# DMA transposes for q, k and the retention output, and four gate groups held back, in a hybrid decoder layer on eight cores

## The chip, the cores and the metric

The kernel runs on all eight cores of one Trainium2 chip. Each core has its own TensorE (PE, matrix multiply into PSUM), VectorE (DVE), ScalarE (ACT), GpSimd (POOL), SyncE (SP) and 16 DMA engines. The metric is the device time in microseconds of the slowest core. The cores do not talk to each other: each computes its own tokens from its own copy of the weights.

## The reference, cut to what matters

```python
h = x @ w_in
a_u, a_v, a_z, r_q, r_k, r_v, r_z, g_a, g_b = split(h)
ya = (spatial_gating(gelu(a_u), gelu(a_v), ...) * silu(a_z)) @ w_oa
q = rotary(r_q); k = rotary(r_k)                  # 8 heads, 128 wide
ret = retention(q, k, r_v)                        # chunks of 128 tokens, v 256 wide
yb = (ret * silu(r_z)) @ w_ob
out = (sigmoid(g_a + b) * ya + sigmoid(g_b + b) * yb) @ w_out
x = layer_norm(2**0.25 * x + out)

# retention, for one head, chunk i, state R
scores = (q k^T) * decay                          # 128 x 128
out_i  = standardize(scores @ v + (q @ R) * cross_decay)
R      = R * chunk_decay + (k * w)^T v
```

x is 4 x 4096 x 2048, so four sequences; each is shared by two cores.

## The kernel before

An even core takes 17 chunks of 128 tokens of a sequence, in tiles of 9 and 8 chunks; an odd core takes the other 15 (tiles of 8 and 7) and first computes the retention state that the even core's chunks leave behind (`prefix`). For each tile the program runs six stages, all of them big matrix products with K = 2048 (16 matmuls of 128 rows into one PSUM bank, called a group): `v_stage`, `uz_stage`, `oa_stage`, `ret_stage`, `obg_stage`, `out_stage`. Weights come by POOL's queue, 512 KB a unit, into a ring of 16 slots (`w_issue`, `w_take`, `w_free`); all other transfers go by SP's queue. Instructions are issued to each engine in the order in which the Python code records them, and `Sched` adds the semaphore waits; a PSUM bank is guarded as a whole between engines.

`ret_stage` is the one that changes. Its main loop has one iteration i for each head h and chunk c, N = 8 x (9 or 8) of them, software-pipelined. In iteration i:

- `p_mm(i)`: the group that makes q, k and v of chunk c, with 512 columns, into a PSUM bank.
- `p_post(i)`: ACT copies q and k (scaled) to `q32` and v to `v`.
- `small_pe(i)`: small matmuls of earlier iterations. For i-2 the two TensorE transposes of q and k (`qkt`, from rotary) into bank 3; for i-4 k^T v (into bank 4); for i-3 the scores (from `qkT`, the transposed q and k); for i-4 the output (from `ST`, `v`, `qkT`, `Rg`) into bank 5 or 6; for i-7 the two TensorE transposes of the normed output `ybp` into bank 7.
- `small_post(i)`: ACT and DVE work behind them: the state `U`, the masked scores `ST`, the norm's statistics `mv`, its factor `rs` (ACT's square root), the normed output `ybp` for i-5, and the ACT copies of the transposes out of PSUM, into `qkT` for i-2 and into `aT` for i-7.
- `rotary(i)`: four DVE operations that write `qkt`, last of DVE's work in the iteration.

The same ring takes in four weight units at each end of a head (`w_free` behind `c == n - 1`).

Behind the loop the gate stage begins: for each of 16 column blocks `ct` a group of r_z, then tanh on ACT and two DVE operations that multiply `aT` by the gate. In its first seven groups the pipeline of the retention runs dry (the drain): each of these has `small_pe` and `small_post` of the iterations N to N+6 between the group and its gate. On ACT a square root and a tanh need different tables, so they cost table loads where they alternate.

```
b = step % 3 if step < 7 + 3 else self.next_bank()
...
if drain:
    small_pe(i)
    small_post(i)
```

Of the kernel before, what the change touches and what calls it, by code (L numbers as in the profile page):

```python
# [9 lines left out]
BF16 = mybir.dt.bfloat16  # L10
AF = mybir.ActivationFunctionType
ALU = mybir.AluOpType
# [3 lines left out]
KT = 16  # L16
NH = 8
CH = 128
# [182 lines left out]
class Prog:  # L201
# [89 lines left out]
    def load(self, key, out, in_, eng="sp", reads=(), after=()):  # L291
        self.S.op(eng, lambda e: e.dma_start(out=out, in_=in_), list(reads), [out], key=key, after=after)  # L292

    def store(self, key, out, in_, eng="sp", writes=()):
        self.S.op(eng, lambda e: e.dma_start(out=out, in_=in_), [in_], list(writes), key=key)

# [248 lines left out]
    def ret_stage(self):  # L545
        m, n = self.m, self.n
# [3 lines left out]
        N = NH * n  # L550
# [8 lines left out]
        def p_mm(i):  # L559
            h, c = divmod(i, n)  # L560
            if c == 0:
                slot[h] = self.w_take(4)
                if init:
                    if h == 0:
                        yh_load(0)
                    if h + 1 < NH:
                        yh_load(h + 1)
            b = i % 3
            s = slot[h]
            self.group(self.bank(b), [(self.xT[:, kt, c * 128:(c + 1) * 128], m.ring[:, s:s + 4, kt, :]) for kt in range(KT)])  # L570
            if c == n - 1:
                self.w_free()

        def p_post(i):
            h, c = divmod(i, n)
            b = i % 3
            q32 = m.q32[i % 3]
            self.act(q32[:, 0, :], self.bank(b)[:, 0:128], AF.Copy, scale=m.dec[:, h:h + 1])
            self.act(q32[:, 1, :], self.bank(b)[:, 128:256], AF.Copy, scale=m.dec[:, 8 + h:9 + h])
            self.act(m.v[i % 6][:], self.bank(b)[:, 256:512], AF.Copy)  # L580

        def rotary(i):
            h, c = divmod(i, n)
            q32, ta, tb = m.q32[i % 3], m.ta[i % 2], m.tb[i % 2]
            x = q32[:].rearrange("p j (e f) -> p (j e) f", e=2)
            cb = m.cs[:, c, 0:64].unsqueeze(1).to_broadcast([128, 4, 64])
            sb_ = m.cs[:, c, 64:128].unsqueeze(1).to_broadcast([128, 4, 64])
            self.tt(ta[:].rearrange("p j e f -> p (j e) f"), x, cb, ALU.mult)
            self.tt(tb[:].rearrange("p j e f -> p (j e) f"), x, sb_, ALU.mult)
            o = m.qkt[i % 6]  # L590
            self.tt(o[:, :, 0:64], ta[:, :, 0, :], tb[:, :, 1, :], ALU.subtract)
            self.tt(o[:, :, 64:128], ta[:, :, 1, :], tb[:, :, 0, :], ALU.add)

        def rg_set(i):
            h, c = divmod(i, n)
# [2 lines left out]
        def state_init(h, b):  # L598
            s = slot[h]
            ps = self.bank(b)[:, 0:256]  # L600
            self.group(ps, [(m.yh[h % 2][:, kt, :], m.ring[:, s + 2:s + 4, kt, :]) for kt in range(KT)])
            self.ts(m.U[:, h, :], ps, float(1.0 / self.gC1[h]), None, ALU.mult)

        def small_pe(i):
            a, b_, c_, y = i - 2, i - 3, i - 4, i - 7
            if 0 <= a < N:
                for j in range(2):
                    self.tr(self.bank16(3)[:, j * 128:(j + 1) * 128], m.qkt[a % 6][:, j, :])
            if 0 <= c_ < N:
                h, c = divmod(c_, n)  # L610
                if not (last and c == n - 1):
                    self.mm(self.bank(4)[:, 128:384], m.qkt[c_ % 6][:, 1, :], m.v[c_ % 6][:], True, True)
            if 0 <= b_ < N:
                self.mm(self.bank(4)[:, 0:128], m.qkT[b_ % 4][:, 1, :], m.qkT[b_ % 4][:, 0, :], True, True)
            if 0 <= c_ < N:
                ob = self.bank(5 + c_ % 2)[:, 0:256]
                self.mm(ob, m.ST[c_ % 3][:], m.v[c_ % 6][:], True, False)
                self.mm(ob, m.qkT[c_ % 4][:, 0, :], m.Rg[c_ % 3][:], False, True)
            if 0 <= y < N:
                for j in range(2):  # L620
                    self.tr(self.bank16(7)[:, j * 128:(j + 1) * 128], m.ybp[y % 4][:, j * 128:(j + 1) * 128])

        def small_post(i):
            a, b_, c_, y = i - 2, i - 3, i - 4, i - 7
            z = i - 5
            if 0 <= z < N:
                k = z % 4
                mv, r = m.mv[k], m.rs[k]
                self.rstd(r[:, 0:1], mv[:, 1:2], m.eps1)
                self.stt(r[:, 1:2], mv[:, 0:1], -1.0, r[:, 0:1], ALU.mult, ALU.mult)  # L630
            if 0 <= a < N:
                self.act(m.qkT[a % 4][:].rearrange("p j t -> p (j t)"), self.bank16(3)[:, 0:256], AF.Copy)
            if 0 <= c_ < N:
                h, c = divmod(c_, n)
                if not (last and c == n - 1):
                    self.stt(m.U[:, h, :], m.U[:, h, :], float(self.gC[h]), self.bank(4)[:, 128:384], ALU.mult, ALU.add)
            if 0 <= b_ < N:
                self.tt(m.ST[b_ % 3][:], self.bank(4)[:, 0:128], m.maskT[:], ALU.mult)
            if 0 <= c_ < N and c_ + 1 < N:
                rg_set(c_ + 1)  # L640
            if 0 <= c_ < N:
                ob = self.bank(5 + c_ % 2)[:, 0:256]
                k = c_ % 4
                self.bn(m.st6[k][:], ob)
                self.aggr(m.mv[k][:, 0:2], m.st6[k][:])
            if 0 <= z < N:
                self.act(m.ybp[z % 4][:], self.bank(5 + z % 2)[:, 0:256], AF.Identity, scale=r[:, 0:1], bias=r[:, 1:2])
            if 0 <= y < N:
                h, c = divmod(y, n)
                self.act(self.aT[:, 2 * h:2 * h + 2, c * 128:(c + 1) * 128],  # L650
                         self.bank16(7)[:, 0:256].rearrange("p (j t) -> p j t", j=2), AF.Copy)

        for i in range(N):
            h, c = divmod(i, n)
            p_mm(i)
            p_post(i)
            small_pe(i)
            if c == 1 and init:
                state_init(h, (i - 1) % 3)
            if i == 3:  # L660
                rg_set(0)
            small_post(i)
            rotary(i)


        i = N
        step = 0
        for ct in range(16):
            s = self.w_take(1)
            for (c0, k) in self.sp:  # L670
                tk = slice(c0 * CH, (c0 + k) * CH)
                drain = i < N + 7
                b = step % 3 if step < 7 + 3 else self.next_bank()
                step += 1
                ps = self.bank(b)[:, 0:k * CH]
                self.group(ps, [(m.ring[:, s, kt, :], self.xT[:, kt, tk]) for kt in range(KT)])
                if drain:
                    small_pe(i)
                    small_post(i)
                    i += 1  # L680
                th = m.zth[self.rot("zt", 4)][:, 0:k * CH]
                self.act(th, ps, AF.Tanh, scale=0.5)
                self.stt(th, th, 1.0, ps, ALU.add, ALU.mult)
                a = self.aT[:, ct, tk]
                self.stt(a, a, 0.5, th, ALU.mult, ALU.mult)
            self.w_free()

    def obg_stage(self):
# [91 lines left out]
def plan_memory(nc, es):  # L780
    m = Mem()
    top = [(nc.sbuf_base + 63) // 64 * 64]
# [30 lines left out]
    m.rs = [new("rs%d" % i, [128, 2], F32) for i in range(4)]  # L813
    m.st6 = [new("st6_%d" % i, [128, 6], F32) for i in range(4)]
    s0 = top[0]
    top[0] += 32768
    assert top[0] <= nc.sbuf_usable_end, (top[0], nc.sbuf_usable_end)
    m.left = nc.sbuf_usable_end - top[0]

# [1 line left out]
    def area(start):  # L821
        pos = [s0 + start]

        def sub(name, shape, dt):
            size = int(np.prod(shape[1:])) * ESIZE[dt]
            off = pos[0]
            pos[0] += (size + 31) // 32 * 32
            assert pos[0] <= s0 + 32768
            return at(name, shape, dt, off)
        sub.pos = pos  # L830
        return sub

    a = area(0)
# [4 lines left out]
    a = area(8192)  # L838
# [5 lines left out]
    a = area(0)  # L844
# [3 lines left out]
    a = area(0)  # L848
# [2 lines left out]
    m.tb = [a("tb%d" % i, [128, 2, 2, 64], F32) for i in range(2)]  # L851
    m.qkt = [a("qkt%d" % i, [128, 2, 128], BF16) for i in range(6)]
    m.v = [a("v%d" % i, [128, 256], BF16) for i in range(6)]
    m.qkT = [a("qkT%d" % i, [128, 2, 128], BF16) for i in range(4)]
    m.ST = [a("ST%d" % i, [128, 128], BF16) for i in range(3)]
    m.ybp = [a("ybp%d" % i, [128, 256], BF16) for i in range(4)]
    m.Rg = [a("Rg%d" % i, [128, 256], BF16) for i in range(3)]
    m.cs = a("cs", [128, NMAX, 128], F32)
    assert a.pos[0] <= s0 + 24576
    a = area(24576)  # L860
    m.zth = [a("zth%d" % i, [128, 512], F32) for i in range(4)]
    a = area(24576)
    m.yh = [a("yh%d" % i, [128, KT, 128], BF16) for i in range(2)]
    a = area(16384)
    m.oga = [a("oga%d" % i, [128, 512], F32) for i in range(2)]
    m.ogb = [a("ogb%d" % i, [128, 512], F32) for i in range(2)]
    a = area(8192)
# [197 lines left out]
```

How the kernel before makes its waits and increments, by code:

```python
    def run(self, name, e):  # L172
        waited = {}
        for o in self.streams[name]:
            need = {}
            for d in o.deps:
                p = self.ops[d]
                sid = id(p.sem)
                if waited.get(sid, 0) < p.count and (sid not in need or need[sid][1] < p.count):
                    need[sid] = (p.sem, p.count)
            for sid, (sem, c) in need.items():
                e.wait_ge(sem, c)
                waited[sid] = c
            if o.fn is None:
                continue
            ins = o.fn(e)
            if o.signal:
                ins.then_inc(o.sem, 16 if o.key is not None else 1)
```

## Time and profile before

| | |
|---|---|
| time, median of 3 runs | 2763.53 us (2761.27 to 2765.18) |
| profiled execution, its time and span | 2764.21 us and 2762.7 us |
| spans of the even cores 0, 2, 4, 6 | 2762.7, 2760.7, 2762.2, 2759.8 us |
| spans of the odd cores 1, 3, 5, 7 | 2689.6, 2691.3, 2691.9, 2699.7 us |
| busy on core 0: PE, DVE, ACT | 97%, 40%, 23% |
| mean granted TensorE clock, core 0 | 0.992 |

The profile is that of core 0, an even core; odd cores are some 70 us shorter, so the even cores set the time. The busy shares are means over all stages. In the retention loop they are another mix than in the rest, and the rows below are taken from it.

### The profile page before, as it was taken

Reading aid. Unit: us, or ns where it says so; the run is one execution under the profiler, and the core shown is the slowest. Engines: PE = TensorE matmul, PEld = TensorE weight load, DVE = VectorE, ACT = ScalarE, POOL = GpSimd, SP = SyncE. Lnnn points to the kernel's source line nnn. Section 1 sums busy time; section 2 is a strip of 40 time slices with the busy share of each in tenths; the row PEclk is TensorE's granted clock in tenths of the full one; section 3 lists DMA queues with packets and bytes.
Section 4 is the critical chain, followed back from the end, with each engine's and each line's share of the span. In section 5 each row is a group of like instructions: output and inputs, shape, how many; then the busy total and the mean of one; then the engine's idle time right before and its main releaser. Section 6 shows DMA issues by size and latency. Waiting matters only on the chain.

```text
span 2762.7 us, 41067 instructions; the slowest of 8 cores (2689.6 to 2762.7 us)
## 1 busy us (share of the span) xinstructions
PE 2691.9 (97%) x14589; PEld 1394.7 (50%) x14666; DVE 1108.6 (40%) x2685; ACT 638.1 (23%) x1516; POOL 197.3 (7%) x373
## 2 busy tenths in 40 slices
PE   5899999999999999999999999999999999999998
PEld 2356666655555666666544444444555544444443
DVE  1344442156665422222375343321566642221257
ACT  0131111045555111111101221110455621111100
POOL 2000000000000000000001000000000000000000
PEclk9999999999999999999999999999999999999999
DMA  9744434423334443333558554444243454444443
GB/s 151 147 78 76 62 62 85 66 42 62 62 62 92 70 84 68 64 71 63 117 185 202 103 92 76 71 83 77 54 78 62 83 94 84 84 69 79 82 124 130
DMA packets 65919, 241.47 MB, mean 87 GB/s; under 512 B 7472, under 2 KB 11696, under 8 KB 62128
## 3 DMA queue, kind: packets, MB, share of 16 engines
q0 software_dynamic: 56064, 193.49, 41.2%
q1 hardware_dynamic: 9648, 45.27, 4.5%
q8 instruction: 125, 2.05, 0.3%
q14 instruction: 82, 0.67, 0.1%
HBM read 413.31 MB, written 18.87 MB: 156 GB/s over the span
## 4 chain that ended last, share of the span: by engine, by line
PE 94%; DMA 3%; ACT 1%; issue 1%; DVE 1%; POOL 0%; SPq 0%; DVEq 0%; ACTq 0%; POOLq 0%
PE ps_all L236 93%; DMA xT<-xT 1%; PE ps_all L245 1%; DMA ring<-w 1%; DMA bgate<-bgate 1%; ACT L257 0%; POOL ring L292 0%; DVE xy_85 L264 0%; ACT aT L257 0%; POOL xT L292 0%; SPq L292 0%; ACT zth_122 L257 0%; DVEq L931 0%; DVE zth_123 L264 0%; DVE wsT L260 0%
## 5 line engine op out<-in xcount | busy, mean ns | idle before, releaser
L236 PE MATMUL ps_all<-xT,ring 128*128 128x384 bf16 (+1 forms) x6343 | 1202.6, 348 | 5.5 <-DVE zth_122 L264 1.8
L236 PEld LDWEIGHTS ps_all<-xT,ring 128*128 128x128 bf16 x6400 | 621.9, 98 | 538.8 <-issue 4.7
L236 PE MATMUL ps_all<-ring,xT 128*128 128x512 bf16 x3264 | 734.7, 382 | 24.1 <-DMA xT<-xT 22.5
L236 PEld LDWEIGHTS ps_all<-ring,xT 128*128 128x128 bf16 x3264 | 314.8, 98 | 386.2 <-issue 37.9
L236 PE MATMUL ps_all<-aT,ring 128*128 128x384 bf16 (+1 forms) x2541 | 482.9, 347 | 1.0
L236 PEld LDWEIGHTS ps_all<-aT,ring 128*128 128x128 bf16 x2560 | 250.1, 98 | 220.0
L292 POOL DMA_DIRECT2D ring<-w x348 | 184.4, 533 | 2434.9 <-PE ps_all L236 1926.9
L236 PE MATMUL ps_all<-ring,yT 128*128 128x512 bf16 x1088 | 235.3, 380 | 0.3 <-DMA ring<-w 0.3
L236 PEld LDWEIGHTS ps_all<-ring,yT 128*128 128x128 bf16 x1088 | 106.3, 98 | 128.9 <-issue 0.8
L275 DVE CAST yT<-ps_all 128x384 bf16<-128x384 f32 (+1 forms) x40 | 24.5, 611 | 205.7 <-PE ps_all L236 205.7
L264 DVE SCALAR_TENSOR_TENSOR ogb_130<-ogb_130,ps_all 128x384 f32<-128x384 f32 (+1 forms) x40 | 24.3, 607 | 183.4 <-PE ps_all L236 183.4
L264 DVE SCALAR_TENSOR_TENSOR ogb_129<-ogb_129,ps_all 128x384 f32<-128x384 f32 (+1 forms) x40 | 24.3, 608 | 183.2 <-PE ps_all L236 183.2
L264 DVE SCALAR_TENSOR_TENSOR uth_77<-uth_77,ps_all 128x384 f32<-128x384 f32 (+1 forms) x40 | 24.3, 608 | 137.1 <-ACT uth_77 L257 113.8
L264 DVE SCALAR_TENSOR_TENSOR uth_76<-uth_76,ps_all 128x384 f32<-128x384 f32 (+1 forms) x40 | 24.3, 608 | 131.8 <-ACT uth_76 L257 82.7
L257 ACT ACTIVATE oga_128<-ps_all,bgate 128x384 f32<-128x384 f32 (+1 forms) x40 | 24.9, 623 | 211.3 <-PE ps_all L236 211.3
L257 ACT ACTIVATE oga_127<-ps_all,bgate 128x384 f32<-128x384 f32 (+1 forms) x40 | 24.9, 623 | 204.7 <-PE ps_all L236 204.7
L257 ACT ACTIVATE yT<-ps_all 128x384 bf16<-128x384 f32 (+1 forms) x40 | 21.3, 533 | 208.3 <-PE ps_all L236 208.3
L257 ACT ACT_TABLE_LOAD x34 | 43.6, 1283 | 98.5 <-PE ps_all L236 54.3
L264 DVE SCALAR_TENSOR_TENSOR oga_128<-oga_128,yT 128x384 f32<-128x384 f32 (+1 forms) x40 | 24.4, 611 | 92.4 <-ACT oga_128 L257 92.4
L264 DVE SCALAR_TENSOR_TENSOR oga_127<-oga_127,yT 128x384 f32<-128x384 f32 (+1 forms) x40 | 24.4, 611 | 90.9 <-ACT oga_127 L257 90.9
L264 DVE SCALAR_TENSOR_TENSOR U<-U,ps_all 128x256 f32<-128x256 f32 x128 | 53.9, 421 | 4.4 <-PE ps_all L236 4.1
L257 ACT ACTIVATE aT<-ps_all 128x256 bf16<-128x256 bf16 x136 | 50.8, 373 | 4.0 <-PE ps_all L245 4.0
(227 smaller groups left out, 1884.5 us busy)
## 6 DMA issues: line engine op xcount, KB each, us to landing
ring<-w POOLq DMA_DIRECT2D x348, 512.0 KB, 6.3
xy_86<-x SPq DMA_DIRECT2D x9, 1024.0 KB, 6.7
out<-xy_86 SPq DMA_DIRECT2D x18, 512.0 KB, 3.8
xy_85<-x SPq DMA_DIRECT2D x8, 1024.0 KB, 4.9
out<-xy_85 SPq DMA_DIRECT2D x16, 512.0 KB, 2.7
xT<-xT POOLq DMA_DIRECT2D x8, 576.0 KB, 22.6
xT<-xT POOLq DMA_DIRECT2D x4, 1024.0 KB, 21.8
ring<-wv POOLq DMA_DIRECT2D x8, 256.0 KB, 19.3
```

Source lines behind the costliest of these rows:

```text
L236: return self.S.op("pe", lambda e: e.matmul(out, lhsT=l, rhs=r, start=start, stop=stop), [l, r], [out])
L245: self.S.op("pe", lambda e: e.transpose(out=out, in_=in_, identity=idt), [in_, idt], [out])
L257: self.S.op("act", lambda e: e.activation(out=out, in_=in_, func=func, **kw), rd, [out])
L264: self.S.op("dve", lambda e: e.scalar_tensor_tensor(out=out, in0=a, scalar=s, in1=b, op0=op0, op1=op1), rd, [out])
L275: self.S.op("dve", lambda e: e.tensor_copy(out=out, in_=in_), [in_], [out])
L292: self.S.op(eng, lambda e: e.dma_start(out=out, in_=in_), list(reads), [out], key=key, after=after)
```

## The change

Three things change, all in `ret_stage`.

First, the four TensorE transposes of an iteration are gone, and the two ACT copies with them. In their place SP's queue gets four DMA transposes of 128 x 128 bf16, SBUF to SBUF: two behind `rotary(i)`, from `qkt` into `qkT`, and two behind the normed output of iteration i-5, from `ybp` straight into `aT`. `qkT` has six buffers where it had four. The readers of `qkT` stay where they were, the scores at i+3 and the output at i+4.

Second, the PSUM banks are dealt anew: `p_mm` rotates over banks 0 to 3 where it had 0 to 2, and k^T v goes into bank 7 where it shared bank 4 with the scores.

Third, the drain: it has four groups where it had seven. These are computed into banks 0 to 3 and held there; `small_pe` and `small_post` of N to N+3 follow each, then `small_post(N+4)`, and only then the gates (tanh and two DVE operations) of the four held groups.

```diff
+    def dma_tr(self, key, out, in_):
+        self.S.op("sp", lambda e: e.dma_start_transpose(out=out, in_=in_), [in_], [out], key=key)
...
-            b = i % 3
+            b = i % 4
...
             self.tt(o[:, :, 64:128], ta[:, :, 1, :], tb[:, :, 0, :], ALU.add)
+            for j in range(2):
+                self.dma_tr("tq%d%d" % (j, i % 6), m.qkT[i % 6][:, j, :], o[:, j, :])
...
         def small_pe(i):
-            a, b_, c_, y = i - 2, i - 3, i - 4, i - 7
-            if 0 <= a < N:
-                for j in range(2):
-                    self.tr(self.bank16(3)[:, j * 128:(j + 1) * 128], m.qkt[a % 6][:, j, :])
...
-            if 0 <= y < N:
-                for j in range(2):
-                    self.tr(self.bank16(7)[:, j * 128:(j + 1) * 128], m.ybp[y % 4][:, j * 128:(j + 1) * 128])
...
-            if 0 <= a < N:
-                self.act(m.qkT[a % 4][:].rearrange("p j t -> p (j t)"), self.bank16(3)[:, 0:256], AF.Copy)
...
-            if 0 <= y < N:
-                h, c = divmod(y, n)
-                self.act(self.aT[:, 2 * h:2 * h + 2, c * 128:(c + 1) * 128],
-                         self.bank16(7)[:, 0:256].rearrange("p (j t) -> p j t", j=2), AF.Copy)
+                for j in range(2):
+                    self.dma_tr("ty%d%d" % (j, z % 4), self.aT[:, 2 * h + j, c * 128:(c + 1) * 128], m.ybp[z % 4][:, j * 128:(j + 1) * 128])
...
-                drain = i < N + 7
-                b = step % 3 if step < 7 + 3 else self.next_bank()
+                b = i - N if i < N + 4 else self.next_bank()
...
+                if i < N + 4:
+                    held.append((ct, c0, k, b))
                     small_pe(i)
                     small_post(i)
                     i += 1
+                    if i == N + 4:
+                        small_post(i)
+                        for g in held:
+                            gate(*g)
+                else:
+                    gate(ct, c0, k, b)
```

On PE one iteration in the middle of the loop read like this before: the group, the q and k transposes (`ident,qkt`), the four small matmuls, the output's transposes (`ident,ybp`).

```order
L236 MATMUL ps_all<-ring,xT 128x512 x16
L245 MATMUL ps_all<-ident,qkt_94 128x128 x2
L236 MATMUL ps_all<-v_104,qkt_98 128x256
L236 MATMUL ps_all<-qkT_107 128x128
L236 MATMUL ps_all<-v_104,ST_111 128x256
L236 MATMUL ps_all<-Rg_118,qkT_106 128x256
L245 MATMUL ps_all<-ident,ybp_114 128x128 x2
```

The same iteration of the changed kernel, with the group of the next behind it:

```order
L236 MATMUL ps_all<-ring,xT 128x512 x16
L236 MATMUL ps_all<-v_104,qkt_98 128x256
L236 MATMUL ps_all<-qkT_111 128x128
L236 MATMUL ps_all<-v_104,ST_113 128x256
L236 MATMUL ps_all<-Rg_120,qkT_110 128x256
L236 MATMUL ps_all<-ring,xT 128x512 x16
```

Four instructions of 128 columns are gone from each iteration; the rest stands in the same order.

On SP nothing stood in the loop before. Now the queue alternates there between the q and k transposes of iteration i and the output's transposes of iteration i-4 (`aT<-ybp` for i-5 stands ahead of `qkT<-qkt` of i):

```order
L295 DMA_TRANSPOSE qkT_110<-qkt_98 128x128 x2
L295 DMA_TRANSPOSE aT<-ybp_115 128x128 x2
L295 DMA_TRANSPOSE qkT_111<-qkt_99 128x128 x2
L295 DMA_TRANSPOSE aT<-ybp_116 128x128 x2
L295 DMA_TRANSPOSE qkT_106<-qkt_94 128x128 x2
```

Four transposes an iteration are issued by one queue, in this order.

On ACT, at the end of the loop and in the drain of the first tile, the order before was this (`rs` is the square root, `zth` the tanh of a gate):

```order
L257 ACTIVATE rs_66<-mv_62,eps_57 128x1
L257 ACTIVATE qkT_108<-ps_all 128x256
L257 ACTIVATE ybp_116<-ps_all,rs_66 128x256
L257 ACTIVATE aT<-ps_all 128x2x128
L257 ACTIVATE zth_121<-ps_all 128x384
L257 ACTIVATE rs_63<-mv_59,eps_57 128x1
L257 ACTIVATE qkT_109<-ps_all 128x256
L257 ACTIVATE ybp_113<-ps_all,rs_63 128x256
L257 ACTIVATE aT<-ps_all 128x2x128
L257 ACTIVATE zth_122<-ps_all 128x384
L257 ACTIVATE rs_64<-mv_60,eps_57 128x1
```

And in the changed kernel:

```order
L257 ACTIVATE rs_63<-mv_59,eps_57 128x1
L257 ACTIVATE ybp_115<-ps_all,rs_63 128x256
L257 ACTIVATE rs_64<-mv_60,eps_57 128x1
L257 ACTIVATE ybp_116<-ps_all,rs_64 128x256
L257 ACTIVATE rs_65<-mv_61,eps_57 128x1
L257 ACTIVATE ybp_117<-ps_all,rs_65 128x256
L257 ACTIVATE rs_66<-mv_62,eps_57 128x1
L257 ACTIVATE ybp_118<-ps_all,rs_66 128x256
L257 ACTIVATE zth_123<-ps_all 128x384
L257 ACTIVATE zth_124<-ps_all 128x384
```

Square roots and tanhs no longer alternate: all the tanhs stand behind the last square root.

## Rows read from the trace of the kernel before

**Rows 1.** The page: the span, and PE's busy time, share and instructions.

```profile
span 2762.7 us, 41067 instructions; the slowest of 8 cores (2689.6 to 2762.7 us)
...
PE 2691.9 (97%) x14589; PEld 1394.7 (50%) x14666; DVE 1108.6 (40%) x2685; ACT 638.1 (23%) x1516; POOL 197.3 (7%) x373
```

**Rows 2.** Windows: the first tile's retention loop, busy time of each engine.

```profile
core 0: us, PE busy (x) PEld busy (x) DVE busy (x) ACT busy (x) POOL busy (x), PEclk, DMA share, GB/s
557.00:845.00 288.00, 288.00 (x1683) 150.28 (x1682) 189.33 (x752) 150.93 (x479) 15.47 (x29) 1.00 0.30 54
```

**Rows 3.** Timeline of PE: start, duration (pipelined, so overlapping), instruction.

```profile
703.39 0.28 PE L245 MATMUL ps_all<-ident,qkt_98 128*128 128x128 bf16 x2
703.50 0.27 PE L236 MATMUL ps_all<-v_102,qkt_96 128*128 128x256 bf16 x1
...
703.89 0.28 PE L245 MATMUL ps_all<-ident,ybp_114 128*128 128x128 bf16 x2
704.00 3.62 PE L236 MATMUL ps_all<-ring,xT 128*128 128x512 bf16 x16
707.45 0.27 PE L245 MATMUL ps_all<-ident,qkt_99 128*128 128x128 bf16 x2
```

**Rows 4.** Line 245, the transposes: count, ns min/median/max, first and last start.

```profile
L245 PE MATMUL ps_all<-ident,ybp_113 x68: 216/220/220, 586.1 to 2205.4; 128*128 128x128 bf16 x68
...
L245 PE MATMUL ps_all<-ident,qkt_99 x44: 218/220/220, 585.7 to 2180.2; 128*128 128x128 bf16 x44
```

**Rows 5.** Waits of PE, whole span: us in total, times, longest.

```profile
PE ps_all L245 <- ACT aT L257: 5.9, 4, 2.0
...
PE ps_all L236 <- DVE zth_122 L264: 1.8, 1, 1.8
PE ps_all L236 <- DVE ST_112 L260: 1.5, 1, 1.5
PE ps_all L236 <- ACT rs_65 L257: 0.8, 1, 0.8
PE ps_all L236 <- DVE ST_111 L260: 0.8, 1, 0.8
```

**Rows 6.** Timeline of PE in the first drain, two gate groups.

```profile
866.29 2.76 PE L236 MATMUL ps_all<-xT,ring 128*128 128x384 bf16 x16
...
871.27 4.38 PE L236 MATMUL ps_all<-xT,ring 128*128 128x384 bf16 x16
```

**Rows 7.** Windows in the first drain, columns as in rows 2 (PEclk is the granted clock).

```profile
872.00:874.00 2.00, 2.00 (x8) 0.89 (x7) 1.11 (x3) 1.33 (x4) 0.00 (x0) 0.50 1.01 203
```

**Rows 8.** Groups by line, ACT from 845 to 892 us.

```profile
L257 ACT ACT_TABLE_LOAD x9 | 11.5, 1283 | 0.2
```

**Rows 9.** Timelines of DVE and ACT, the iteration of rows 3.

```profile
704.83 0.16 DVE L289 RECIPROCAL rs_66<-rs_66 128x1 f32<-128x1 f32 x1 [0.94 <-ACT rs_66 L257]
...
707.40 0.49 DVE L260 TENSOR_TENSOR qkt_94<-ta_90,tb_92 128x128 bf16<-128x128 f32 x2
...
705.35 0.56 ACT L257 ACTIVATE ybp_116<-ps_all,rs_66 128x256 bf16<-128x256 f32 x1 [0.35 <-DVE rs_66 L264]
```

**Rows 10.** Timeline of SP's queue at the start: issue time, duration of the issue.

```profile
48.33 0.57 SPq L292 DMA_DIRECT2D dec<-dec  x1
...
50.27 0.66 SPq L292 DMA_DIRECT2D bgate<-bgate  x1
```

**Rows 11.** DMA issues by line: count, KB each, median us from issue to landing.

```profile
out<-xy_85 SPq DMA_DIRECT2D x16, 512.0 KB, 2.7
...
dec<-dec SPq DMA_DIRECT2D x1, 8.0 KB, 15.7
...
bgate<-bgate SPq DMA_DIRECT2D x1, 16.0 KB, 25.7
```

**Rows 12.** Timeline of POOL, the weight loads behind one head.

```profile
700.10 2.11 POOL L292 DMA_DIRECT2D ring<-w  x4 [34.43 <-PE ps_all L245]
```

**Rows 13.** Windows behind it, columns as in rows 2.

```profile
704.00:706.00 2.00, 2.00 (x13) 0.94 (x11) 1.06 (x6) 1.65 (x7) 0.00 (x0) 1.00 1.05 211
...
710.00:712.00 2.00, 2.00 (x14) 1.15 (x13) 1.75 (x7) 0.42 (x2) 0.00 (x0) 1.00 1.05 213
712.00:714.00 2.00, 2.00 (x13) 0.99 (x11) 0.89 (x5) 1.65 (x7) 0.00 (x0) 1.00 0.22 43
```

More of the change, by code:

```diff
@@ L575, in p_post @@
             h, c = divmod(i, n)
-            b = i % 3
+            b = i % 4
             q32 = m.q32[i % 3]
@@ L604, in small_pe @@
         def small_pe(i):
-            a, b_, c_, y = i - 2, i - 3, i - 4, i - 7
-            if 0 <= a < N:
-                for j in range(2):
-                    self.tr(self.bank16(3)[:, j * 128:(j + 1) * 128], m.qkt[a % 6][:, j, :])
+            b_, c_ = i - 3, i - 4
             if 0 <= c_ < N:
@@ L611, in small_pe @@
                 if not (last and c == n - 1):
-                    self.mm(self.bank(4)[:, 128:384], m.qkt[c_ % 6][:, 1, :], m.v[c_ % 6][:], True, True)
+                    self.mm(self.bank(7)[:, 0:256], m.qkt[c_ % 6][:, 1, :], m.v[c_ % 6][:], True, True)
             if 0 <= b_ < N:
-                self.mm(self.bank(4)[:, 0:128], m.qkT[b_ % 4][:, 1, :], m.qkT[b_ % 4][:, 0, :], True, True)
+                self.mm(self.bank(4)[:, 0:128], m.qkT[b_ % 6][:, 1, :], m.qkT[b_ % 6][:, 0, :], True, True)
             if 0 <= c_ < N:
@@ L617, in small_pe @@
                 self.mm(ob, m.ST[c_ % 3][:], m.v[c_ % 6][:], True, False)
-                self.mm(ob, m.qkT[c_ % 4][:, 0, :], m.Rg[c_ % 3][:], False, True)
-            if 0 <= y < N:
-                for j in range(2):
-                    self.tr(self.bank16(7)[:, j * 128:(j + 1) * 128], m.ybp[y % 4][:, j * 128:(j + 1) * 128])
+                self.mm(ob, m.qkT[c_ % 6][:, 0, :], m.Rg[c_ % 3][:], False, True)
         def small_post(i):
-            a, b_, c_, y = i - 2, i - 3, i - 4, i - 7
-            z = i - 5
+            b_, c_, z = i - 3, i - 4, i - 5
             if 0 <= z < N:
@@ L635, in small_post @@
                 if not (last and c == n - 1):
-                    self.stt(m.U[:, h, :], m.U[:, h, :], float(self.gC[h]), self.bank(4)[:, 128:384], ALU.mult, ALU.add)
+                    self.stt(m.U[:, h, :], m.U[:, h, :], float(self.gC[h]), self.bank(7)[:, 0:256], ALU.mult, ALU.add)
             if 0 <= b_ < N:
@@ L646, in small_post @@
             if 0 <= z < N:
+                h, c = divmod(z, n)
                 self.act(m.ybp[z % 4][:], self.bank(5 + z % 2)[:, 0:256], AF.Identity, scale=r[:, 0:1], bias=r[:, 1:2])
-            if 0 <= y < N:
-                h, c = divmod(y, n)
-                self.act(self.aT[:, 2 * h:2 * h + 2, c * 128:(c + 1) * 128],
-                         self.bank16(7)[:, 0:256].rearrange("p (j t) -> p j t", j=2), AF.Copy)
+                for j in range(2):
+                    self.dma_tr("ty%d%d" % (j, z % 4), self.aT[:, 2 * h + j, c * 128:(c + 1) * 128], m.ybp[z % 4][:, j * 128:(j + 1) * 128])
         for i in range(N):
@@ L658, in ret_stage @@
             if c == 1 and init:
-                state_init(h, (i - 1) % 3)
+                state_init(h, (i - 1) % 4)
             if i == 3:
@@ L663, in ret_stage, with gate @@
             rotary(i)
+        def gate(ct, c0, k, b):
+            tk = slice(c0 * CH, (c0 + k) * CH)
+            ps = self.bank(b)[:, 0:k * CH]
+            th = m.zth[self.rot("zt", 4)][:, 0:k * CH]
+            self.act(th, ps, AF.Tanh, scale=0.5)
+            self.stt(th, th, 1.0, ps, ALU.add, ALU.mult)
+            a = self.aT[:, ct, tk]
+            self.stt(a, a, 0.5, th, ALU.mult, ALU.mult)
         i = N
-        step = 0
+        held = []
+        self.nbank = 4
         for ct in range(16):
@@ L670, in ret_stage @@
             for (c0, k) in self.sp:
-                tk = slice(c0 * CH, (c0 + k) * CH)
-                drain = i < N + 7
-                b = step % 3 if step < 7 + 3 else self.next_bank()
[L674 to L677, printed above, removed]
+                b = i - N if i < N + 4 else self.next_bank()
+                self.group(self.bank(b)[:, 0:k * CH], [(m.ring[:, s, kt, :], self.xT[:, kt, c0 * CH:(c0 + k) * CH]) for kt in range(KT)])
+                if i < N + 4:
+                    held.append((ct, c0, k, b))
                     small_pe(i)
@@ L680, in ret_stage @@
                     i += 1
[L681 to L685, printed above, removed]
+                    if i == N + 4:
[4 more added lines that the diff above has]
+                    gate(ct, c0, k, b)
             self.w_free()
@@ L815, in plan_memory @@
     s0 = top[0]
-    top[0] += 32768
+    top[0] += 34816
     assert top[0] <= nc.sbuf_usable_end, (top[0], nc.sbuf_usable_end)
@@ L827, in sub @@
             pos[0] += (size + 31) // 32 * 32
-            assert pos[0] <= s0 + 32768
+            assert pos[0] <= s0 + 34816
             return at(name, shape, dt, off)
@@ L853, in plan_memory @@
     m.v = [a("v%d" % i, [128, 256], BF16) for i in range(6)]
-    m.qkT = [a("qkT%d" % i, [128, 2, 128], BF16) for i in range(4)]
+    m.qkT = [a("qkT%d" % i, [128, 2, 128], BF16) for i in range(6)]
     m.ST = [a("ST%d" % i, [128, 128], BF16) for i in range(3)]
@@ L858, in plan_memory @@
     m.cs = a("cs", [128, NMAX, 128], F32)
-    assert a.pos[0] <= s0 + 24576
-    a = area(24576)
+    assert a.pos[0] <= s0 + 26624
+    a = area(26624)
     m.zth = [a("zth%d" % i, [128, 512], F32) for i in range(4)]
-    a = area(24576)
+    a = area(26624)
     m.yh = [a("yh%d" % i, [128, KT, 128], BF16) for i in range(2)]
```

## The prediction

> **What bounds the kernel now.** I read the spans first: the profile is core 0's, the slowest, and PE is busy for 2691.9 of its 2762.7 us [rows 1], so time can only come from PE's own work or its waits. Then the windows of the stage that changes: in the first tile's retention loop PE is busy for 288 of 288 us, DVE for 189 and ACT for 151 [rows 2]. The chain there is PE alone; ACT's copies and DVE's operations are off it, and shortening them gains nothing by itself. Then PE's timeline of one iteration: from one q/k transpose pair to the next is 707.45 - 703.39 = 4.06 us [rows 3]. The waits last: PE has none in the loops, and five kinds in the two drains [rows 5].
>
> **What the change removes from PE.** A transpose reads as 220 ns [rows 4], but that is its latency; successive matmuls overlap. What it costs is the distance to the next start: the q/k pair takes 703.50 - 703.39 = 0.11 us, the output's pair 704.00 - 703.89 = 0.11 us [rows 3]. There are 544 on this core: four buffers of the output with 68 each, and six of q/k with 46 or 44 [rows 4], which is two pairs in each of 136 iterations. So 136 x 0.22 = 29.9 us, and an iteration becomes 3.84 us. PE has no wait in the loop that could swallow this. DVE is the next engine: in each iteration it waits 0.94 us for ACT's square root [rows 9], so it could follow down to about 3.1 us. ACT loses two copies and has more room still.
>
> **What the drain gives.** PE's waits there are 5.9 (for the ACT copies into `aT`, behind table loads), 1.8, 1.5, 0.8 and 0.8 us, together 10.8 [rows 5]. Nine table loads of 1.28 us lie between 845 and 892 us [rows 8], because square roots and tanhs alternate. Behind these waits the granted clock was 0.50, the 1.2 GHz level, and one gate group took 4.38 instead of 2.76 us [rows 6, 7]: 1.6 us more. In the new order one switch to tanh is left, nothing on PE reads an ACT copy of a transpose, and the four held banks let PE go on; banks 4 to 7 serve the next four groups while DVE works off the held gates. Of the 12.4 us I take 10; the rest may go to the last q/k transposes. Those have less time than in the loop: two gate groups of 2.76 us with their small matmuls, less 0.45 us, about 5.5 us.
>
> **What it adds.** 544 DMA transposes, four an iteration, issued by SP in one order, each of 32 KB. On SP's queue in these loops nothing stands behind them but themselves, so a late one delays only the later ones; PE waits for the q/k pair, and the gates much later for the output's. Nothing in this trace shows a transpose by DMA, so its cost is bounded by its neighbours, on three counts.
>
> First the latency. `qkt` of an iteration is complete at 707.40 + 0.49 = 707.89, 4.5 us behind its group's end at 703.39 [rows 3, 9]. The scores that read the transpose are three groups on, at 703.39 + 3 x 3.84 + 0.1 = 715.0. That leaves 7.1 us. The quickest landing in the rows is 2.7 us, for a 512 KB store [rows 11]; two transposes, with the output's pair ahead of them, still fit 7.1 us. The output's pair is ready at 705.91 [rows 9] and nobody on PE waits for it. Cost: 0.
>
> Second the rate. Four an iteration fit if each takes the queue less than 3.84 / 4 = 0.96 us. From below, an issue on SP's queue takes 0.57 to 0.66 us [rows 10], so 2.3 to 2.6 us for four, hidden behind the 3.84 us of PE. From above, if they ran one at a time at 2.7 us from issue to landing [rows 11], an iteration would be 10.8 us, 136 x (10.8 - 3.84) = 947 us more. DMAs on one queue do not wait for each other's landing: the loads of the start were issued 0.6 us apart and landed one behind the other [rows 10, 11]. So I take the lower bound, nearer to a 32 KB transfer with no HBM in it. VectorE: DVE Perf Modes of the Trainium skill, section "The three transpose paths", speaks against that: it gives 1309 ns for a 128 x 128 bf16 transpose by DMA. If that were time on the queue and not latency, an estimate by it is 4 x 1.31 = 5.24 us an iteration, 136 x 1.40 = 190 us more, a time near 2914. No run here shows which of the two it is.
>
> Third the company of the weight loads. Four units are issued at each end of a head [rows 12], and the DMA engines are then full until about 713 us [rows 13], some 11.5 us. At the start of the kernel, beside a full weight queue, three loads of 128 short rows in a row landed from 48.33 + 15.7 = 64.0 (`dec`) to 50.27 + 25.7 = 76.0 us (`bgate`): 4.0 us each for 8 to 16 KB [rows 10, 11]. They were slow by their number of rows, not by their bytes. A transpose also reads 128 rows, of 256 bytes. At 4.0 us each, only three or four of them pass in such a stretch. From below, if its rows travel together, it takes well under a microsecond beside the loads too. I take the lower bound here as well, with less confidence: those loads came from HBM, and at a time when the queue had been full for 40 us.
>
> **The sum.** 2764.2 (this execution; 0.7 over the median of 2763.5) - 29.9 - 10 = 2724.3 us. With all 12.4 us of the drain it is 2722; with no drain gain and a microsecond lost in each of 14 heads it is 2748. So the forecast's own range is 2718 to 2748.
>
> **Rival 1: the weight loads delay the transposes.** Count from a group's end E, as at 699.3. The loads are issued 0.8 us later and fill the engines from about E + 1.8. The output's pair enters at E + 2.5, and at 4.0 us each it ends at E + 10.5. The next q/k pair, entered at E + 4.3, would end near E + 15, when the loads (stretched a little by sharing) are done. PE needs it at E + 4.3 + 7.1 = 11.4: a wait of about 4 us, once a head. There are 14 such stretches in the loops (the last of each tile falls into the drain), and in each a wait of that size may be followed by a drop to the lower clock, as in the first drain, 1.6 us. That is 56 to 78 us, and some 10 more in the two drains, in place of the gain there: 2764 - 30 + 66 to 88 = 2800 to 2822. At 2 us a wait and no clock loss it is 2764 - 30 + 28 = 2762. I call it 2790. It decides against the change from about 2.2 us a head. For it: the short-row loads. Against it: the transposes' source is SBUF. DMA: Bandwidth & Descriptors of the Trainium skill, section "Queues, rings and completion order", says that each DMA engine takes turns between queues packet by packet; the 4.0 us of those loads agree with it, if a row is a packet. Whether a transpose's rows are packets of their own no run here shows.
>
> **Rival 2: the transposes are too slow in themselves,** above 0.96 us of queue each. Each 0.1 us above is 4 x 0.1 x 136 = 54 us, so it is worse than before from 1.03 us on, and can reach 2724 + 947 = 3670. For it: a transpose may have to end before the next one begins, which no row here can show. Against it: the 0.57 to 0.66 us of an issue. Its likeliest part lies at 2830 to 2950.
>
> **Rival 3: the time on PE comes back.** DVE's chain starts only when ACT's square root is done, and PE's small matmuls need DVE's results of the iteration before; if that loop closes at more than 3.84 us, the iteration stays near 4.06 and only the drain is won: 2754 to 2764. The 0.94 us of DVE's wait speak against it.
>
> **Chances and range.** Forecast 0.45, rival 1 0.32, rival 2 0.18, rival 3 0.05. A measurement of this kernel can tell about 0.2%, 5.5 us, from no change. Faster by more: the forecast, a fifth of rival 1 and half of rival 3, 0.53. Within: 0.06. Slower: 0.41. The range of 8 in 10 holds the forecast, rivals 1 and 3 up to where the clock loss is counted in full, and the edge of rival 2: 2716 to 2840. The forecast's own range, 2718 to 2748, holds somewhat under half.
>
> **What would show it.** Right: iterations 3.84 us apart on PE, PE busy for the whole loop, transposes landing within 7 us of issue also beside weight loads, no more than one or two table loads in a drain, no clock drop there. Rival 1: PE waiting for a DMA into `qkT` once a head, some microseconds behind POOL's four loads, and nowhere else. Rival 2: the same wait in every iteration, and SP's queue never idle in the loop. Rival 3: iterations of 4 us with PE waiting for DVE or ACT. The forecast is wrong if a transpose takes more than a quarter of an iteration, alone or in company.

## The result and the profile after

The changed kernel takes 2951.18 us (median of three runs, 2949.97 to 2954.36) against 2762.4: the ratio is 1.0685, 95% interval [1.0664, 1.0706]. Executions in a slower state of the chip, in which the cores of one die show a lower clock (here one of four, at 3299.09 us), are left out of this time and of those below. The kernel is 6.9% slower where 1.4% faster was forecast, and it lies outside the range of 2716 to 2840. The mechanisms that did it are rivals 2 and 1 of the prediction, both at once.

The page of the profile after, for core 6: the span, PE, and the packets of the queue that SP issues on.

```profile
span 2952.8 us, 41929 instructions; the slowest of 8 cores (2850.5 to 2952.8 us)
PE 2719.9 (92%) x14122; PEld 1375.6 (47%) x14122; DVE 1110.7 (38%) x2685; ACT 543.6 (18%) x1228; POOL 197.4 (7%) x373
...
q1 hardware_dynamic: 96688, 63.16, 7.8%
```

PE does 544 matmuls less than in [rows 1] (by its weight loads, 14122 against 14666) and is busy for 28 us more, so it ran slower; and for 233 us of the span it is idle, where it was 71 us. Its waits over the whole span say for what:

```profile
PE ps_all L236 <- DMA qkT_109<-qkt_97: 56.0, 8, 10.8
PE ps_all L236 <- DMA qkT_107<-qkt_95: 38.9, 10, 11.7
PE ps_all L236 <- DMA qkT_106<-qkt_94: 36.7, 8, 9.8
PE ps_all L236 <- DMA qkT_111<-qkt_99: 25.7, 6, 9.6
...
PE ps_all L236 <- DVE U L264: 6.3, 3, 2.2
PE ps_all L236 <- DMA qkT_110<-qkt_98: 6.0, 5, 2.0
PE ps_all L236 <- DMA qkT_108<-qkt_96: 3.2, 3, 1.1
```

The six buffers of `qkT` add up to 166.5 us in 40 waits. In PE's timeline 18 of them, 3.75 to 11.72 us long, make 145 us of it, and each of these ends 6 to 18 us after POOL has issued weight loads. None of the waits of [rows 5] on `aT` copies, `ST` or `zth` is left.

The cause shows on SP's queue. The line of the transposes (durations are of the issue, ns min/median/max), and the time to landing:

```profile
L295 SPq DMA_TRANSPOSE qkT_107<-qkt_95 x46: 1093/1184/1840, 564.3 to 2374.7; - x46
...
DMA to landing us min/median/max: 2.2/2.4/12.9
```

An issue takes SP 1.18 us, where a plain load's took 0.57 to 0.66 [rows 10]. The timeline of SP's queue around the stall at 690 us (start, duration of two issues together):

```profile
683.28 2.37 SPq L295 DMA_TRANSPOSE qkT_111<-qkt_99  x2
685.80 2.40 SPq L295 DMA_TRANSPOSE aT<-ybp_118  x2
688.39 2.46 SPq L295 DMA_TRANSPOSE qkT_106<-qkt_94  x2
691.00 3.05 SPq L295 DMA_TRANSPOSE aT<-ybp_115  x2
```

From 683.28 to 688.39 are 5.1 us for four transposes: the queue rests here for no more than 0.2 us between two pairs, and with this order an iteration can't stay shorter than that. PE's timeline beside it, its waits in brackets:

```profile
676.69 0.22 PE L236 MATMUL ps_all<-qkT_109 128*128 128x128 bf16 x1 [0.98 <-DMA qkT_109<-qkt_97]
...
681.87 0.22 PE L236 MATMUL ps_all<-qkT_110 128*128 128x128 bf16 x1 [1.06 <-DMA qkT_110<-qkt_98]
...
686.98 0.22 PE L236 MATMUL ps_all<-qkT_111 128*128 128x128 bf16 x1 [1.02 <-DMA qkT_111<-qkt_99]
...
701.25 0.27 PE L236 MATMUL ps_all<-qkT_106 128*128 128x128 bf16 x1 [9.85 <-DMA qkT_106<-qkt_94]
...
701.75 5.56 PE L236 MATMUL ps_all<-ring,xT 128*128 128x512 bf16 x16
```

Three iterations 5.1 us apart, each with a wait of 1.0 us: that is the issue. Then one wait of 9.85 us. It lies behind the four weight loads, which POOL issues here:

```profile
686.45 2.12 POOL L292 DMA_DIRECT2D ring<-w  x4 [48.84 <-PE ps_all L236]
```

And the group behind that wait takes 5.56 us in place of 3.62 [rows 3]. The windows (columns as in rows 2) show why:

```profile
692.00:694.00 2.00, 0.00 (x0) 0.00 (x0) 0.69 (x3) 1.27 (x5) 0.00 (x0) 1.00 1.06 202
694.00:696.00 2.00, 0.00 (x0) 0.00 (x0) 0.00 (x0) 0.10 (x1) 0.00 (x0) 0.86 1.05 200
696.00:698.00 2.00, 0.00 (x0) 0.00 (x0) 0.00 (x0) 0.00 (x0) 0.00 (x0) 0.50 1.09 205
...
702.00:704.00 2.00, 2.00 (x6) 0.72 (x5) 1.65 (x7) 0.00 (x0) 0.00 (x0) 0.50 0.15 33
```

PE stands idle, the granted clock falls to 0.50 (1.2 GHz), and it is still there when PE works again. So the sum for the loss of 190 us is: 166.5 of waits on `qkT`, some 9 on DVE behind them (`U` above, two of 1.4 us on `rs`), 28 + 30 = 58 of PE time at the lower clock, less 30 of transposes and 11 of the old drain's waits: 193. The 58 us are found by subtraction: PE was busy 28 us longer with 30 us less of work.

Behind the long wait PE's scores and SP's queue go on like this:

```profile
707.26 0.22 PE L236 MATMUL ps_all<-qkT_107 128*128 128x128 bf16 x1
...
722.64 0.22 PE L236 MATMUL ps_all<-qkT_111 128*128 128x128 bf16 x1
727.76 0.22 PE L236 MATMUL ps_all<-qkT_106 128*128 128x128 bf16 x1 [1.03 <-DMA qkT_106<-qkt_94]
```

```profile
704.77 2.37 SPq L295 DMA_TRANSPOSE qkT_109<-qkt_97  x2
710.33 2.37 SPq L295 DMA_TRANSPOSE aT<-ybp_118  x2
```

The queue has caught up: it rests for 3.2 us, from 707.14 to 710.33. PE then runs five iterations in a row, 3.84 us apart, without a wait, before the issue holds it up again at 727.76. So a long wait pays in advance for some of the short ones, and where a wait stands does not tell which of the two causes it would go with; for that the causes have to be taken away one at a time.

### The profile page after: what moved, and what is told of

Same layout as the page of the kernel before. It is cut to its first block, busy times and chain, and to the rows that moved or that the text cites. A ratio compares the mean times of both kernels' runs of the same rounds, so it can differ in the third digit from the quotient of the medians.

```text
span 2952.8 us, 41929 instructions; the slowest of 8 cores (2850.5 to 2952.8 us)
## 1 busy us (share of the span) xinstructions
PE 2719.9 (92%) x14122; PEld 1375.6 (47%) x14122; DVE 1110.7 (38%) x2685; ACT 543.6 (18%) x1228; POOL 197.4 (7%) x373
## 3 DMA queue, kind: packets, MB, share of 16 engines
q1 hardware_dynamic: 96688, 63.16, 7.8%
## 4 chain that ended last, share of the span: by engine, by line
PE 81%; DMA 9%; SPq 6%; issue 1%; DVE 1%; ACT 1%; POOL 0%; DVEq 0%; ACTq 0%; POOLq 0%
PE ps_all L236 81%; SPq L295 6%; DMA qkT_109<-qkt_97 2%; DMA qkT_107<-qkt_95 2%; DMA qkT_106<-qkt_94 1%; DMA xT<-xT 1%; DMA bgate<-bgate 1%; DMA qkT_111<-qkt_99 1%; DMA ring<-w 1%; POOL ring L292 0%; DVE xy_85 L264 0%; DMA qkT_110<-qkt_98 0%; SPq L182 0%; DMA qkT_108<-qkt_96 0%; ACT q_2_89 L257 0%
## 5 line engine op out<-in xcount | busy, mean ns | idle before, releaser
L236 PE MATMUL ps_all<-ring,xT 128*128 128x512 bf16 x3264 | 766.4, 393 | 24.8 <-DMA xT<-xT 20.6
L236 PEld LDWEIGHTS ps_all<-ring,xT 128*128 128x128 bf16 x3264 | 328.0, 101 | 416.4 <-issue 83.3
L257 ACT ACTIVATE q_1_88<-ps_all,dec 128x128 f32<-128x128 f32 x90 | 28.3, 364 | 182.4 <-PE ps_all L236 182.4
```

What stands on the lines that cost most here:

```text
L236: return self.S.op("pe", lambda e: e.matmul(out, lhsT=l, rhs=r, start=start, stop=stop), [l, r], [out])
L257: self.S.op("act", lambda e: e.activation(out=out, in_=in_, func=func, **kw), rd, [out])
```

## The experiments

**Merged pairs.** Is it the instruction or the data that costs the issue?

```diff
-            for j in range(2):
-                self.dma_tr("tq%d%d" % (j, i % 6), m.qkT[i % 6][:, j, :], o[:, j, :])
+            self.dma_tr("tq%d" % (i % 6), m.qkT[i % 6][:], o[:].rearrange("p j t -> p (j t)"))
...
-                for j in range(2):
-                    self.dma_tr("ty%d%d" % (j, z % 4), self.aT[:, 2 * h + j, c * 128:(c + 1) * 128], m.ybp[z % 4][:, j * 128:(j + 1) * 128])
+                self.dma_tr("ty%d" % (z % 4), self.aT[:, 2 * h:2 * h + 2, c * 128:(c + 1) * 128], m.ybp[z % 4][:])
```

> The changed kernel with each pair of transposes as one DMA transpose of 128 x 256, so two issues an iteration in place of four. Theory A (SP's time for an issue, 1.18 us each, is paid per instruction): two issues take 2.4 us of a 3.84 us iteration, SP's queue has idle time, and the waits of every iteration go; 2724 to 2750 if the weight loads do no harm. Theory B (an issue's time goes by the data, 16 blocks of 16 x 128 now where there were 8): each issue takes about 2.4 us, an iteration stays at 5.1 us, and the time stays at 2950. Theory C (the rows of a transpose share the DMA engines with the weight loads): whatever the issue costs, PE still waits for qkT once a head, behind POOL's four loads, for 4 to 10 us: 2790 to 2860 if the issue is cheap.

Measured: 2831.32 us, ratio 1.0242 [1.0225, 1.0259]. The issue of a transpose twice as large, then PE's wait:

```profile
L295 SPq DMA_TRANSPOSE qkT<-qkt x136: 1167/1169/2459, 562.4 to 2256.0; - x136
...
PE ps_all L236 <- DMA qkT<-qkt: 72.3, 20, 5.0
```

1.17 us for 128 x 256 as for 128 x 128: theory A on the issue, B falls. What remains are 20 waits instead of 40, about one a head, in the place that theory C gives; 18 of them are 2.5 to 5.0 us long, at the lower end of its 4 to 10 us. PE's timeline and POOL's:

```profile
686.97 0.27 PE L236 MATMUL ps_all<-qkT 128*128 128x128 bf16 x1 [4.39 <-DMA qkT<-qkt]
727.10 0.22 PE L236 MATMUL ps_all<-qkT 128*128 128x128 bf16 x1 [3.81 <-DMA qkT<-qkt]
```

```profile
671.57 2.11 POOL L292 DMA_DIRECT2D ring<-w  x4 [38.45 <-PE ps_all L236]
712.21 2.11 POOL L292 DMA_DIRECT2D ring<-w  x4 [38.53 <-PE ps_all L236]
```

These two waits end some 15 us after the loads were issued.

**The changed kernel without the weight loads of the loops.** The edit leaves out the loads (POOL has 64 fewer, 284 of 348), so later heads and the first gates use old weights:

```diff
-                self.w_free()
+                self.wissued = self.wpos + NSLOT
```

> The changed kernel without the weight loads that are issued at the ends of heads (the ring keeps old weights there, so later heads and the first gate blocks compute with the wrong ones; the instructions are the same). Theory A (issue time): the loops still run at four issues, 5.1 us an iteration, PE waits for qkT about 1.2 us in each: 2860 to 2900. Theory C (sharing with the weight loads alone): the waits go, 2724 or a little less.

Measured: 2901.57 us (one run). PE's wait:

```profile
PE ps_all L236 <- DMA qkT<-qkt: 130.1, 105, 3.5
```

105 waits of 1.24 us in the mean, in place of 40 with 18 long ones: the issue bound by itself, as theory A has it, with nothing of the loops' weight loads in it. The time is 1.6 us above its range.

**Both taken away.** Merged pairs and no loads in the loops (with old weights in the same places):

> The kernel with merged pairs, without the weight loads at the ends of heads (old weights stay in the ring, so later heads and the first gate blocks compute with the wrong ones; the instructions are the same). With issue cost and sharing both gone nothing is left of the loss: no PE wait for qkT in the loops and 2722 to 2728. If waits remain, a third cause is at work.

Measured: 2717.2 us (one run). No wait on `qkT` is left, and no sign of a third cause. It is 5 us under the lower end of what was expected; the cause stays open. The four kernels make a square of spans: 2952.8 as changed, 2899.3 without loads, 2828.8 merged, 2714.9 with both. The issue costs 184 us where there are no loads, the loads 114 us where there is no issue bound; together they cost 238, not 298. The 60 us between are overlap, and the timeline above shows one way of it: in the five iterations behind a long wait the issue costs PE nothing.

**One pair alone.** The output's pair by DMA, q and k on TensorE as before, the new drain kept:

```diff
+            if 0 <= a < N:
+                for j in range(2):
+                    self.tr(self.bank16(3)[:, j * 128:(j + 1) * 128], m.qkt[a % 6][:, j, :])
...
+                self.act(m.qkT[a % 6][:].rearrange("p j t -> p (j t)"), self.bank16(3)[:, 0:256], AF.Copy)
```

> The changed kernel with the q/k transposes back on TensorE and their ACT copy back; only the output's pair goes by DMA, and the drain with four held groups stays. No instruction on PE waits for a DMA transpose. All theories: two issues of 1.2 us an iteration fit; PE saves 0.11 us x 136 = 15 us, and the drain's 10 to 12 us: 2737 to 2742.

Measured: 2735.54 us (median of three runs, 2733.99 to 2738.98), ratio 0.990 [0.988, 0.992]. That is 1.5 us under what was expected. Its transposes land as late as 13.2 us, and PE doesn't wait for them.

And the reverse, q and k by DMA in the kernel before, two issues an iteration:

> The kernel before with only the q/k pair by DMA; the output's transposes, their ACT copies and the old drain of seven groups stay. Two issues of 1.2 us an iteration leave SP's queue idle for more than a third of it. Theory A (issue time alone): no wait in the loops, 15 us saved, 2749. Theory C (sharing with the weight loads): once a head, behind POOL's four loads, PE waits for qkT, some 2 to 8 us and in places a drop of the clock behind it: 14 heads, 2780 to 2860. Waits in every iteration speak against both.

Measured: 2813.63 us, ratio 1.0179 [1.0162, 1.0196]. PE's wait:

```profile
PE ps_all L236 <- DMA qkT<-qkt: 50.3, 21, 4.6
```

Theory C: the issue fits with room, and once a head PE still waits, mostly for 2 to 5 us. It is the pair that PE reads soon that does the harm.

**Deeper pipeline.** With merged pairs, the readers of `qkT` two iterations later:

```diff
-            b_, c_ = i - 3, i - 4
+            b_, c_ = i - 5, i - 6
...
-            b_, c_, z = i - 3, i - 4, i - 5
+            b_, c_, z = i - 5, i - 6, i - 7
...
-                if i < N + 4:
+                if i < N + 6:
```

> The kernel with merged pairs, and the readers of qkT two iterations later (scores at i-5, output at i-6; seven buffers of qkt, v and qkT, two of ST and Rg, six groups in the drain). Slack of a q/k transpose 14.8 us in place of 7.1; the longest landing with merged pairs was 14.7 us. Theory (only the lateness of one pair a head costs): the waits of PE go and the time is 2722 to 2740. Rival (the DMA engines lose throughput beside the loads, so that lateness adds up): waits remain, 2770 or more.

Measured: 2724.56 us, ratio 0.9862 [0.9843, 0.9882]: the fastest of the kernels that load all their weights, and 1.4% under the kernel before. The landing times (min/median/max), the one wait left on `qkT`, then POOL's four loads and PE's timeline some 11 to 15 us behind them:

```profile
DMA to landing us min/median/max: 2.3/3.7/14.6
...
PE ps_all L236 <- DMA qkT<-qkt: 2.6, 1, 2.6
```

```profile
657.52 2.11 POOL L292 DMA_DIRECT2D ring<-w  x4 [31.96 <-PE ps_all L236]
...
668.38 0.22 PE L236 MATMUL ps_all<-qkT 128*128 128x128 bf16 x1
...
672.21 0.22 PE L236 MATMUL ps_all<-qkT 128*128 128x128 bf16 x1
```

The transposes are as late as with merged pairs alone, up to 14.6 us, and with a slack of 14.8 us PE waits for none of them in the loops (the 2.6 us lie in a drain): iterations stand 3.83 us apart. So the loads make single transposes late and do not take throughput that is missed.

The same depth with four transposes an iteration:

> The deep pipeline (readers of qkT two iterations later) with four transposes an iteration, as the changed kernel has them. The issue bound does not care for slack: four issues of 1.18 us and the gaps between them make an iteration of 5 us once the slack is used up, whatever the depth: 2870 to 2920. If depth alone were the cure, it would be 2724 as with merged pairs.

Measured: 2904.0 us, ratio 1.0512 [1.0493, 1.0531]. PE waits 137.8 us for `qkT`. Depth takes 47 us off the changed kernel, about what leaving out the loads takes off (50), and no more: it doesn't help against a bound of 5.1 us an iteration.

**Pacing the weight loads.** The first try, with merged pairs:

> The kernel with merged pairs, and the four weight loads of a head paced: one unit behind every second chunk of the next head, none before the drain's held groups are through. Each load then fills the DMA engines for some 2.6 us in place of 11. Sharing theory (the four loads in a row are what makes the transposes late): a q/k transpose is late by less than its slack of 7 us, PE's waits for qkT go, no clock drops: 2722 to 2735. Rival (the transposes disturb by their number, or any load beside them is too much): waits of PE for qkT of a microsecond or more stay in each head, 2760 and more.

Measured: 3205.75 us, ratio 1.1593 [1.157, 1.1616]. The edit was at fault: it loaded a head's own ring slots anew while the head still used them, so the head went on with other weights, and PE waited 352.7 us for them. It says nothing on pacing. Put right:

```diff
-            if c == n - 1:
-                self.w_free()
+            self.w_issue(self.wpos - 8 + (c + 1) // 2 + NSLOT, after=[len(self.S.ops) - 1])
...
-            self.w_free()
+            if ct >= 2:
+                self.w_free()
```

> The pacing of the weight loads again, with the edit put right (the faulty one loaded a head's own slots anew while it still used them, and PE waited for weights): the kernel with merged pairs, the pipeline as deep as in the changed kernel, the four units that a finished head frees loaded one by one behind every second chunk of the next head, none before the held groups are through. Sharing theory: PE's waits for qkT shrink from 72 us to under 5, no clock drops, 2720 to 2732. Rival: waits of a microsecond or more stay in each head: 2750 and more.

Measured: 2755.46 us (median of nine runs, 2749.62 to 2762.94), ratio 0.9968 [0.9941, 0.9995]. PE's wait:

```profile
PE ps_all L236 <- DMA qkT<-qkt: 20.3, 10, 6.4
```

The waits shrink from 72.3 to 20.3 us, so the four loads in a row were most of the harm. They don't go, and the time lies in the range of the rival. But PE's timeline has only six of the ten waits in the loops, 0.2 to 2.1 us each and 5.3 us together. The other four, 15.1 us, lie in the two drains, and there the edit does not do what it was meant to. In the first drain (the first held group, POOL's loads, a wait):

```profile
838.86 2.76 PE L236 MATMUL ps_all<-xT,ring 128*128 128x384 bf16 x16
...
839.24 1.07 POOL L292 DMA_DIRECT2D ring<-w  x2 [3.37 <-PE ps_all L236]
840.92 1.06 POOL L292 DMA_DIRECT2D ring<-w  x2 [0.61 <-issue]
...
848.98 0.27 PE L236 MATMUL ps_all<-qkT 128*128 128x128 bf16 x1 [4.27 <-DMA qkT<-qkt]
```

POOL issues four units within 3 us while the held groups have just begun: `if ct >= 2` moves them back in POOL's own order, but a load waits only for its slot of the ring, and the last head has freed its slots. So in the loops pacing did nearly what the sharing theory says, and most of what is left is again loads in a row. Of the rival this remains: in the loops a single load beside merged pairs can still use up the 7 us of slack and cost up to 2 us. In the place of one such wait, of 1.0 us, the windows show the DMA engines at a share of 1.25 with only 60 GB/s, so their packets took time that the bytes don't account for; what took it is left open:

```profile
600.00:604.00 4.00, 2.97 (x16) 1.39 (x15) 2.86 (x13) 1.65 (x5) 0.53 (x1) 1.00 1.25 60
```

Paced and deep together:

> Merged pairs, deep pipeline and paced loads together. The deep kernel has one wait of 2.6 us left on qkT, in a drain, and the kernel without loads was at 2717: 2717 to 2724, at most 0.3% under the deep one.

Measured: 2732.53 us (median of three runs, 2729.74 to 2738.35), ratio 0.9884 [0.9862, 0.9905]: above what was expected, and not better than depth alone. PE waits 10.9 us for `qkT` in three places, the longest 6.6 us. All three lie in the two drains, at whose start POOL has again issued four or five units within 3 us; in the loops no wait on `qkT` is left.

**The drain by itself.** The output's pair by DMA, with the gates at once behind their groups:

```diff
-                b = i - N if i < N + 4 else self.next_bank()
+                b = step % 3 if step < 8 else self.next_bank()
+                step += 1
...
-                if i < N + 4:
-                    held.append((ct, c0, k, b))
+                if i < N + 5:
```

> The kernel with only the output's pair by DMA, with the drain of the kernel before: gates at once behind each group, groups on banks 0 to 2, five groups that carry the pipeline's rest. It measures the drain's part by itself. Theory: holding the gates is worth the 10 to 12 us that were worked out from PE's waits, so 2747 to 2751. Rival: the drain's waits came mainly from the ACT copies of the output's transposes, which are gone here too, so it is 2739 to 2743.

Measured: 2742.39 us, ratio 0.992 [0.9901, 0.994], against 0.990 with the held gates; the intervals overlap, the runs (2740.91 to 2742.97 against 2733.99 to 2738.98) do not. By PE's waits the old order has 7.7 us in its drains (on `zth`, `U` and `rs`), the held one 3.8 (on `rs` and `qkT`). The spans of the two profiled executions, 2740.4 and 2734.0 us, are 6.4 us apart. So holding the gates is worth some 4 to 7 us, less than the 10 to 12 of the theory, and the time is in the rival's range.

## Why the prediction was wrong, step by step

**PE's saving: right.** Iterations that don't wait are 3.83 us apart, as worked out.

**The drain: right in sum.** The deep merged kernel has both terms and nothing of the loss but 2.6 us, and takes 2724.56 us where the sum gave 2724.3; that it is so close is in part luck, since its drain holds six groups and not four. The prediction gave one sum for the held gates and the lost copies together. The last experiment, which gave all 10 to 12 us to the gates, found some 4 to 7 for them; about as much goes with the copies into `aT`, whose waits were 5.9 us [rows 5].

**The rate: the step that failed.** "So I take the lower bound": an issue of 0.57 to 0.66 us, read from plain loads. A transpose's issue takes 1.09 us at least and 1.18 in the median, four of them with their gaps 5.1 us, over the 3.84 us of an iteration. The sum had nothing for this term; it costs 184 us where there are no loads. The threshold of 0.96 us was right, the row that stood for the unseen operation was not. The 1309 ns that VectorE: DVE Perf Modes of the Trainium skill gives ("The three transpose paths") are near the 1.18 us measured as time on the queue, and the estimate worked out by it, 2914, was near the 2901.6 of the kernel without loads. The prediction left open whether that figure is time on the queue or latency and went by the lower bound all the same; the latency alone is 2.3 us.

**The company of the weight loads: the second step that failed,** also by taking the lower bound. Rival 1 gave a wait of about 4 us a head from the three short-row loads; the merged kernel shows 2.5 to 5.0 in most of its waits, and the loads cost it 114 us. The question that was left open, whether a transpose's rows are packets of their own, the page of the profile bears on. That queue's line before, and with merged pairs:

```profile
q1 hardware_dynamic: 9648, 45.27, 4.5%
...
q1 hardware_dynamic: 87984, 63.13, 8.5%
```

(96688 - 9648) / 544 = 160 packets a transpose; with merged pairs (87984 - 9648) / 272 = 288. That is 128 or 256 and 32 more, as if each row of 256 bytes were a packet. The rule of DMA: Bandwidth & Descriptors of the Trainium skill ("Queues, rings and completion order"), that each DMA engine takes turns between queues by packets, would fit the waits here. That the loads make the transposes late is shown by taking them away; that turns by packets are the way, no run shows, nor whether the profile counts the same packets as that page.

**The latency: right.** 2.2 to 2.4 us where nothing stands in the way.

**Rival 3 did not come.** DVE followed to 3.83 us.

**The price of a wait was too small.** Rival 1 counted 1.6 us of lower clock for a wait. In the changed kernel PE's work at the lower clock costs 58 us beside 166 of waits; put down to the 18 long ones alone it is 3.2 us for each. In the merged kernel PE is busy for 36 us more than in the same kernel without loads (2691.7 against 2655.6), 1.8 us for each of 20 waits.

## What to carry to other kernels

A DMA transpose has a price on the queue that issues it, here 1.2 us an instruction for 128 x 128 and for 128 x 256 alike: count the issues in an iteration against its length, and make few large ones. Behind the issue comes the landing, which beside other loads took up to some 15 us for what takes 2.3 alone (23.8 us at the longest in the paced and deep kernel). So a result that the busy engine reads needs that much slack, or should be one that it reads only much later, as the output's pair. Here a deeper pipeline gave the slack (2724.6 us); pacing the loads came less far (2755.5 us), and most of the waits that it left lay in the drains, which it did not reach. Two causes that share one slack cost less together than apart, so it takes runs without each of them to price them. An operation that the trace does not show deserves the dearer of its bounds until it has been run once.

## What the runs showed of the hardware

The issue of a 128 x 128 transpose took 1.09 us at least and 1.18 in the median, that of a 128 x 256 one 1.17 us. A transpose made 160 or 288 packets on the profile's page. Alone it landed in 2.3 us, beside four weight loads in up to 12.9 us (128 x 128, the changed kernel) and 14.7 us (128 x 256, merged pairs); without the loops' loads the latest took 6.4 and 6.1 us. In the changed kernel each of PE's 18 waits of 3.75 us and more was followed by a group that took 5.0 to 6.3 us, where a group of 512 columns takes 3.62 otherwise [rows 3]; in the one whose windows are shown the granted clock was 0.50, the 1.2 GHz level.
